# Four expert slots to a step in two places, the first operation of a short convolution on ScalarE, and products ahead of scores

## The reference, cut to what matters

```python
# first block, gated short convolution, width 3 over positions
u = cg * xc
conv = conv_b + sum(conv_w[j] * up[:, j:j + s] for j in range(3))
y_conv = bg * conv
# first block, attention: 16 heads of 64, softmax over the band, all 512 tokens visible backwards
probs = softmax(q k^T * scale + bias);  out = probs v
gates = sigmoid(h w_gate + b_gate)
# second block, the expert layer: 8 heads x 16 = 128 experts of 16384 for each token
act = gelu(einsum('td,tkd->tk', xb, expert_u[idx]))
y = einsum('tk,tkd->td', gate * act, expert_v[idx])
```

## Time and profile before

| | us |
|---|---|
| runs before, median of 3 (lowest, highest) | 2625.08 (2621.37, 2626.10) |
| the profiled execution, its own time | 2623.89 |
| its span | 2621.4 |
| TensorE matmul busy | 2131.6 (81%) |
| TensorE weight load busy | 1609.0 (61%) |
| VectorE busy | 1721.2 (66%) |
| ScalarE busy | 668.9 (26%) |
| POOL busy | 798.8 (30%) |
| DMA, mean over the span | 305 GB/s |

### The profile page before, as it was taken

The page is one execution under the profiler, slowest core; times in us unless marked ns, Lnnn a source line. Parts: engine busy times, 40 slices in busy tenths (PEclk is TensorE's granted clock), DMA queues, the critical chain, the costliest instruction groups (busy, mean ns, idle before and its releaser), DMA issues. The chain is left out here.

```text
span 2621.4 us, 26327 instructions
## 1 busy us (share of the span) xinstructions
PE 2131.6 (81%) x9024; PEld 1609.0 (61%) x9024; DVE 1721.2 (66%) x3608; ACT 668.9 (26%) x1575; POOL 798.8 (30%) x541
## 2 busy tenths in 40 slices
PE   8999999999999999897999989997554454454454
PEld 6787788888888778676888878876111111121121
DVE  4662110000427679687787668777999999999997
ACT  2103302102442410563231135632211111111110
POOL 0000000000001244234443322235754565555651
PEclk9999999999999999999999999999767777777876
DMA  6774434443345699799999986578999999999997
GB/s 259 264 302 130 137 113 147 158 147 126 113 145 219 269 384 407 274 332 341 371 420 421 419 309 225 209 294 343 422 421 422 421 422 421 421 390 422 421 422 299
DMA packets 114868, 798.33 MB, mean 305 GB/s; under 512 B 13328, under 2 KB 16528, under 8 KB 19248
## 3 DMA queue, kind: packets, MB, share of 16 engines
q0 software_dynamic: 74736, 540.57, 50.8%
q1 hardware_dynamic: 40000, 256.09, 26.3%
HBM read 790.27 MB, written 6.34 MB: 304 GB/s over the span
## 5 line engine op out<-in xcount | busy, mean ns | idle before, releaser
L604 PE MATMUL PS<-reg,ring 128*128 128x256 f32 x6016 | 1361.5, 385 | 39.9 <-DVE reg L1877 7.1
L604 PEld LDWEIGHTS PS<-reg,ring 128*128 128x128 f32 x6016 | 1148.2, 193 | 219.0 <-issue 41.6
L552 POOL DMA_INDIRECT uv<-in_expert_uv,experts x329 | 529.1, 1608 | 1579.7 <-DVE experts L1587 824.9
L1634 DVE SCALAR_TENSOR_TENSOR acc<-uv,coef,acc 128x1024 f32<-128x1024 f32 x261 | 335.3, 1285 | 9.6 <-DVE coef L1617 0.3
L579 PE MATMUL PS<-uv,spare 128*128 128x512 f32 x260 | 171.4, 809 | 161.7 <-ACT spare L1075 161.7
L1605 DVE CUSTOM_DVE_ANT_0 uv<-uv,h_tok 128x1024 f32<-128x1024 f32 x225 | 267.3, 1219 | 29.1 <-DMA uv<-in_expert_uv,experts 28.7
L579 PE MATMUL PS<-reg,spare 128*128 128x512 f32 x212 | 129.4, 755 | 138.4 <-ACT spare L1075 138.4
L1082 ACT ACTIVATE acts<-dots 128x2 f32<-128x2 f32 (+2 forms) x194 | 39.6, 204 | 744.1 <-DVE dots L1605 704.4
L579 PEld LDWEIGHTS PS<-uv,spare 128*128 128x128 f32 x260 | 63.0, 257 | 267.1 <-issue 267.1
L552 POOL DMA_INDIRECT reg<-in_expert_uv,experts x107 | 153.5, 1435 | 116.2 <-PE PS L579 73.8
L579 PEld LDWEIGHTS PS<-reg,spare 128*128 128x128 f32 x212 | 49.0, 246 | 219.8 <-issue 219.8
(11 more groups left out here) (264 smaller groups left out, 2088.8 us busy)
## 6 DMA issues: line engine op xcount, KB each, us to landing
ring<-in_weights SPq DMA_DIRECT2D x228, 1024.0 KB, 5.9
uv<-in_expert_uv,experts POOLq DMA_INDIRECT x329, 15.6
kv_half<-reg SPq DMA_DIRECT2D x1, 2052.0 KB, 10.8
reg<-kv_half SPq DMA_DIRECT2D x1, 2052.0 KB, 13.1
reg<-in_x_t SPq DMA_DIRECT2D x2, 1024.0 KB, 5.5
reg<-in_sub_t SPq DMA_DIRECT2D x2, 1024.0 KB, 4.8
toep<-rel_neg SPq DMA_DIRECT2D x16, 128.0 KB, 6.5
x_tokens<-reg SPq DMA_DIRECT2D x2, 1024.0 KB, 9.9
```

The source lines that it names most:

```text
L552: gp.indirect_dma_start(UV[r], None, a["expert_uv_2"], bass.IndirectOffsetOnAxis(ap=experts[:, e % 256:e % 256 + 1], axis=0))\
L604: mm = pe.matmul(out_tile(n, t), w[:, t * P:(t + 1) * P], mv, start=first and k == order[0], stop=last and k == order[-1])
L1634: dve.scalar_tensor_tensor(acc[:, :], v, c, acc[:, :], ALU.mult, ALU.add).then_inc(acc_done, 1)
```

## The change

Groups of the slots 148 to 179 are four slots instead of two. `APART` marks each group whose predecessor is such a group; its step takes two places: at the first the coefficients and additions of the group before (and the routing of a list and its exponential, if one is due), at the second the four dot products and the Gelu. The places by block are these:

| place after | before: adds, dots | after: adds, dots |
|---|---|---|
| K2 0 | 146-147, 148-149 | 146-147, 148-151 |
| K2 1 | 148-149, 150-151 | 148-151, none |
| QKM 0 | 150-151, 152-153 | none, 152-155 |
| QKM 2 | 152-153, 154-155 | 152-155, none |
| V2 0 and 1, VM, OM (two each for a block) | two and two | four dots, four adds, in turn |
| OM 1 (end) | 172-173, 174-175, list 12 | 172-175, none, list 12 |
| WO2 0 | 174-175, 176-177 | none, 176-179 |
| WO2 1 | 176-177, 178-179 | 176-179, none |
| WO2 2 | 178-179, 180-181 | none, 180-181 |
| PQ 0 | 180-181, 182-183 | the same |

In the short convolution of both halves the first operation of each tile goes from VectorE to ScalarE (`conv_start`), into one of four tiles of `spare`; VectorE waits for it on a new semaphore `conv_head`. In the attention of both halves TensorE does the six fill products of item 0 ahead of the scores of item 0, and waits for the banks by lane, one lane ahead of item 0, the other three ahead of items 1 and 2; the fill of item 0 in the loop is gone.

```diff
+FOUR = ((148, 180),)
+IN_FOURS = set(itertools.chain(*(range(a, b) for a, b in FOUR)))
-GROUPS = [(s, s + 2) for s in range(0, 2 * NSLOT, 2)] + [(s, s + 4) for s in range(2 * NSLOT, NS - 4, 4)] \
+GROUPS = [(s, s + (4 if s in IN_FOURS else 2)) for s in range(0, 2 * NSLOT, 2) if s not in IN_FOURS or s % 4 == 0] + [(s, s + 4) for s in range(2 * NSLOT, NS - 4, 4)] \
+APART = [s0 - 1 in IN_FOURS for s0, _ in GROUPS]
-STEPS = sum(TICKS) + 4 + len(MORE)
+_ends = list(itertools.accumulate(1 + apart for apart in APART))
+STEPS = _ends.index(sum(TICKS) + 4 + len(MORE)) + 1
+def late(g):
+
+    return g + 1 < NG and APART[g + 1]
...
# TensorE, expert_steps
+                    if g < NG and APART[g]:
+                        yield
                     yield
# TensorE, attention
-                for i in range(4):
-                    for t in range(2):
-                        evac_wait(pe, NO[hf, BG, i], t)
...
                 fill = fill_products()
+                for _ in range(PER_ITEM):
+                    next(fill)
+                free = {LANE[NO[hf, BG, i]][t]: (i, t) for i in range(4) for t in range(2)}
+                evac_wait(pe, NO[hf, BG, free[0][0]], free[0][1])
                 scores(0)
+                for lane in (1, 2, 3):
+                    evac_wait(pe, NO[hf, BG, free[lane][0]], free[lane][1])
                 scores(1, 2)
                 for i in range(N_ITEMS):
-                    for _ in range(PER_ITEM // 2):
+                    for _ in range(PER_ITEM // 2 if i else 0):
                         next(fill)
...
# ScalarE, expert_steps
+                    if g < NG and APART[g]:
+                        for item in ROUTED_AT[g - 1]:
+                            gate_exps(item)
+                        yield
                     if g < NG:
                         s0, s1 = GROUPS[g]
                         act.wait_ge(dot_done, s1)
...
-                        for item in ROUTED_AT[g]:
-                            gate_exps(item)
+                        if not late(g):
+                            for item in ROUTED_AT[g]:
+                                gate_exps(item)
                     yield
# ScalarE, half
-                only_ticks(hf, XC, BG)
+                def conv_start(j):
+                    evac_wait(act, NO[hf, XC, j // 2], j % 2)
+                    if j >= 4:
+                        evac_wait(act, NO[hf, BG, (j - 4) // 2], j % 2)
+                    act.activation(spare[:, j % 4, :], UC[:, j, 2:T + 2], ACT.Identity, scale=col("conv_w", 16 + j),
+                                   bias=col("conv_b", j)).then_inc(conv_head, 1)
+
+                tick(hf, XC, 0)
+                for i in range(1, 4):
+                    tick(hf, XC, i)
+                    conv_start(i - 1)
+                conv_start(3)
+                for i in range(4):
+                    settle()
+                    for t in range(2):
+                        if i < 2:
+                            conv_start(4 + 2 * i + t)
+                    tick(hf, BG, i)
# VectorE, expert_steps
+                    if g < NG and APART[g]:
+                        for item in ROUTED_AT[g - 1]:
+                            routed_item = item
+                            routing(item)
+                        yield
                     if g < NG:
                         dot_products(g)
...
# VectorE, half
-                        c, at = tmp[:, j % 2, :], 8 * hf + j
+                        c, at = spare[:, j % 4, :], 8 * hf + j
                         evac_wait(dve, NO[hf, XC, i], t)
-                        if j >= 2:
-                            evac_wait(dve, NO[hf, BG, (j - 2) // 2], t)
-                        dve.tensor_scalar(c, UC[:, j, 2:T + 2], col("conv_w", 16 + j), col("conv_b", j), ALU.mult, ALU.add)\
-                            .then_inc(conv_a, 1)
-                        dve.wait_ge(conv_a, 2 * at + 1)
+                        dve.wait_ge(conv_head, at + 1)
                         dve.scalar_tensor_tensor(c, UC[:, j, 1:T + 1], col("conv_w", 8 + j), c, ALU.mult, ALU.add)\
                             .then_inc(conv_a, 1)
```

More of the change, by code:

```diff
@@ L1 @@
+import itertools
 from contextlib import ExitStack
@@ L352, in build @@
             "sq_done", "ms_done", "rt_done", "rr_done", "hb_done", "hn_done"))
-        halved, carried, conv_a, conv_b = sem("halved"), sem("carried"), sem("conv_a"), sem("conv_b")
+        halved, carried, conv_head, conv_a, conv_b = (sem(n) for n in ("halved", "carried", "conv_head", "conv_a", "conv_b"))
         toep_loaded = [sem("toep_loaded0"), sem("toep_loaded1")]
@@ L1068, in expert_steps @@
                     if g:
-                        act.wait_ge(coef_done, g)
                         for s in range(*GROUPS[g - 1]):
@@ L1072, in expert_steps @@
                                 n = PE_NO[s]
+                                act.wait_ge(coef_done, g)
                                 if n >= 4:
@@ L1684, in expert_steps @@
                             top_list(1, j, 32 + j)
-                        for item in ROUTED_AT[g]:
-                            routed_item = item
-                            routing(item)
+                        if not late(g):
+                            for item in ROUTED_AT[g]:
+                                routed_item = item
+                                routing(item)
                     yield
@@ L1850, in half @@
                         j = 2 * i + t
-                        c, at = tmp[:, j % 2, :], 8 * hf + j
+                        c, at = spare[:, j % 4, :], 8 * hf + j
                         evac_wait(dve, NO[hf, XC, i], t)
-                        if j >= 2:
-                            evac_wait(dve, NO[hf, BG, (j - 2) // 2], t)
-                        dve.tensor_scalar(c, UC[:, j, 2:T + 2], col("conv_w", 16 + j), col("conv_b", j), ALU.mult, ALU.add)\
-                            .then_inc(conv_a, 1)
-                        dve.wait_ge(conv_a, 2 * at + 1)
+                        dve.wait_ge(conv_head, at + 1)
                         dve.scalar_tensor_tensor(c, UC[:, j, 1:T + 1], col("conv_w", 8 + j), c, ALU.mult, ALU.add)\
                             .then_inc(conv_a, 1)
-                        dve.wait_ge(conv_a, 2 * at + 2)
+                        dve.wait_ge(conv_a, at + 1)
                         dve.scalar_tensor_tensor(c, UC[:, j, 0:T], col("conv_w", j), c, ALU.mult, ALU.add).then_inc(conv_b, 1)
```

## The result

| | us |
|---|---|
| before, median of 4 runs (lowest, highest) | 2624.26 (2621.37, 2626.10) |
| after, median of 4 runs (lowest, highest) | 2601.55 (2599.59, 2603.78) |
| ratio, 95% interval | 0.9915 (0.9902 to 0.9929) |
| profiled execution after: own time, span | 2599.59, 2597.9 |
| forecast for it | 2610.5 |

The change made the kernel 22.3 us faster by the ratio (18.6 to 25.7). The forecast was 13.4 us, and the range ended at 2604.0: the sign was right, and some 9 us of gain were missing from the sum.

The account below looks back on a forecast made before the run. TensorE was taken to bound half 1, DMA the later stretch of expert slots alone. The terms 8.2 + 1.0 + 0.4 + 2.6 + 1.2 = 13.4 us gave 2610.5 for the profiled execution, 2611.7 from the median; range 2604 to 2619.5.

Parts of the forecast that it names:

- part 1: Convolution's first operation on ScalarE and fill ahead of scores: 8.2 us in half 1 and 1.0 us in half 0.
- part 2: Four-slot steps: 0.4 us in QKM, 2.6 us at WO2 and 1.2 us of clock behind it.
- Table loads: Place steps: eight Gelus and about six of 13 table loads go; counted as nothing, hidden in ScalarE's idle time.
- Part 1, half 1: End of BG into the scores: 8.2 us saved, 4.7 of TensorE idle time and 3.5 of slow clock.
- Part 1, half 0: End of BG: idle time of 0.79 us goes and the 18 fill instructions run faster, 1.0 us saved.
- QKM: Four dots at QKM 0 instead of two and two shorten the place ahead of the 5.00 us idle time: 0.4 us.
- WO2 and the clock behind it: TensorE's idle time of 3.10 us shrinks to 0.5, saving 2.6 us; faster clock in the 32 instructions behind, 1.2 us.
- Mixers, DMA, the last stretch: Mixers gain nothing, hidden under TensorE's work; gathers land in time; the slots-alone stretch, 1820 to 2614, keeps its length.
- Rival C: Removed Gelus and table loads lie on the path after all: 9.3 us more gain, 2602.4 us; chance 0.07.
- Rivals A and B: Half 1: softmax or DMA leaves 2 of 8.2 us (2617.9, chance 0.15), or ScalarE starts convolution late (2620, chance 0.08).
- Rival B: Half 1: ScalarE starts the convolution late, held by an owed Gelu; about 3 us gained there, 2620; chance 0.08.
- Rival D: Gathers come late for fourth dots, beyond a 14.7 us limit; at 20 us landing time, 2644.5 us; chance 0.05.

Follow-up runs that it names:

- e16: The changed kernel measured again, nothing altered: 2599.49 us.
- e7: Changed kernel without slots in fours and with ScalarE's coef_done wait back ahead of the slot loop: 2608.05 before is e6's; this one took 2611.42 us.
- e9: Kernel before, with ScalarE's coef_done wait moved into the branch only for groups 21 to 36 (attention of half 1): 2615.11 us.
- e11: Kernel before, waits unchanged, with the Gelu table loaded ahead of both waits for groups 21 to 36: 2619.69 us, runs in two groups.
- e12: Kernel before, with only the fill ahead of the scores and its waits by lane, coef_done wait kept: 2614.86 us.
- e8: Kernel before, with only the slots in fours, coef_done wait kept ahead of the loop: 2617.86 us.
- e6: Changed kernel with only ScalarE's coef_done wait put back ahead of the slot loop: 2608.05 us.
- e5: Kernel before, with only ScalarE's coef_done wait moved from ahead of the slot loop into the branch for slots TensorE adds: 2609.45 us.
- e10: Kernel before, with ScalarE's coef_done wait moved for every group but 21 to 36: 2620.30 us.
- e15: Changed kernel with slots 76 to 179 in fours instead of 148 to 179: 2610.64 us.
- e1: Changed kernel with convolution and fill order undone, keeping the slots in fours and the moved coef_done wait: 2606.56 us.

## Why the prediction was wrong, point by point

- **The failed step** is a term that the sum 8.2 + 1.0 + 0.4 + 2.6 + 1.2 leaves out: it goes through part 1 and part 2 of the diff and has no item for the line that both share. The paragraph "Table loads" asked only how many loads go away, and said "I count nothing", because ScalarE has idle time. It did not ask where a load stands to the wait in front of it. In the attention, ScalarE has idle time too (29.0 us ahead of 13 loads in the kernel before), but it is idle time spent ahead of the load, while everything behind hangs on it. The wait moved is worth 11.3 us alone and 22.3 - 14.4 = 7.9 on top of the rest (9.5 with e16 in place of the first measurement). Of the missing 9 us this term is 8, and the other is the 14.4 against the 13.4 that was added up. The paragraph's smaller reading was off as well: about six loads were to go, and 5 went.
- **Part 1, half 1:** 8.2 us forecast, 8.0 on the timeline, and 10.2 for both halves in e7 against 9.2. Right, mechanism and size. Two details were off and cost nothing: the operation takes 0.60 us and not 0.47, and VectorE ends BG 2.7 us behind TensorE where I wanted at most 1, because it got some 1.8 us ahead and not 3.5 (1055.27 to 1049.06, less TensorE's 4.5). The fill covers it.
- **Part 1, half 0:** 1.0 us forecast. The idle time is gone, and the lead grows from 1.0 us in the first products to 1.8 us at the end of the attention of half 0 (314.86 to 313.05), so about 0.8.
- **QKM:** 0.4 forecast, and 0.7 in the row (5.00 to 4.34).
- **WO2 and the clock behind it:** 2.6 + 1.2 forecast. The idle time of 3.10 us went wholly, and the clock behind it gave 10.01 - 8.83 = 1.2, as taken. From the end of the idle time of 2.03 us ahead of WO2 to the start of the 32 instructions behind it the profile has 35.3 us instead of 39.7. So the timeline has 4.4 for the 2.6, but the profile of before is a slow one here: e7, e9, e11 and e12, whose expert steps there are also in twos and whose wait stands as before, have 38.3 to 38.5 us, and 9.1 to 9.6 for the 32 instructions. Against these it is 3.0 to 3.3, and 0.3 to 0.7 for the clock. In the runs the fours as a whole are 3.7 (e8), or 14.4 - 10.2 = 4.2 (e6 against e7), which is the forecast.
- **Mixers, DMA, the last stretch:** no idle time of TensorE that was not there before, the idle time in the mixers' first step is 2.09 for 2.15, and the last stretch is the same. Right.
- **Rival C** gives 2602.4, next to the measured 2601.55, and is still wrong. It put the surplus on the loads and Gelus that the fours remove, 9.3 us more than the forecast. e8 has the fours, with all these loads removed, and is worth 3.7 us. The surplus comes from loads that stay and stand in another place, in a stretch without fours. The Trainium skill (ScalarE: Activation LUTs, What ACT_TABLE_LOAD costs) counts 2.66 us for a switch, of which 1.28 are the load. This case's trace agrees on the load and not on the rest. Where ScalarE goes straight from one function to another, in the kernel before, a switch takes 1.32 us in all, from the end of the one operation at 1080.67 to the start of the next at 1081.99, and the measurement decides:

```profile
1080.47 0.20 ACT L1082 ACTIVATE acts<-dots 128x2 f32<-128x2 f32 x1
1080.69 1.28 ACT L1218 ACT_TABLE_LOAD   x1
1081.99 0.62 ACT L1218 ACTIVATE reg<-reg,norms 128x384 f32<-128x384 f32 x1
```

- **Rivals A and B** fell: part 1 kept its 8 us, and the scores start right behind the fill. (Rival B's time does not follow from its own terms: with 3 us for part 1 in half 1 the sum is 8.2, so 2616.9 and not 2620.) **Rival D** did not show either: from K2 to WO2 VectorE's longest waits are for TensorE and ScalarE, 7.7 us the largest in all, and no gather is among them. But it came nearer than the text had it: in the stretch of the second line of the earlier trace rows the gathers now land after 10.4 us (median) and 13.5 at most, where 14.7 was the limit.

What stays open: how the terms add. The moved wait is 11.3 alone, 12.6 on top of the fours, 7.6 on top of part 1 and 7.9 or 9.5 on top of both, and the intervals of some 3 us and more each way do not say how much of this is overlap. Some is likely, since in e5 the two idle times that the parts remove are already shorter: 3.57 us at the end of BG instead of 4.68, and 2.14 ahead of WO2's last sums instead of 3.10.

Single profiles are a coarse measure for terms of this size. The idle time ahead of half 1's first projections ends between 977.0 and 982.0 us in the profiles of before, e5, e9, e10 and e11. Even the stretch from there to the end of the attention, with the same instructions, takes 214.0, 215.5 and 217.7 us (changed kernel, e16, e15), 223.5 and 224.7 (e5, e1), 223.6 and 227.1 (e7, e6), and 231.6 and 231.1 (before, e8). So the step from the wait kept to the wait moved is larger than this spread with and without part 1, but a difference of 2 or 3 us between two profiles is nothing.

## What to carry to other kernels

Go through a diff by its lines and not by its description, and give a moved wait a term of its own, even if the description does not mention it: ask for each engine which instruction now carries which wait. A table load that stands behind a wait is paid at every place where someone hangs on the function behind it; put it, or the wait, so that the engine loads while it would wait anyway, and look for rows in which a wait is ended ahead of a table load. Fewer loads by larger groups are not the same thing: in the attention of this kernel that made it 8 us slower.
